# Moving one store, one mask load and eight key multiplies and transposes in a two-layer decoder kernel

## The reference

```python
k_cmp = rms_norm(compress(kc_all, prm['cw_k'][li]), prm['kn_c'][li, 0])
s = jnp.einsum('bqhgd,bnhd->bqhgn', q_blk, k_cmp).astype(jnp.float32) * ATTN_SCALE
```

## Time and profile before

| | |
|---|---|
| median of three runs | 1782.42 us (1781.62 to 1784.81) |
| the profiled execution | 1780.31 us, span 1778.4 us |
| TensorE busy | 1699.6 us (96%) |
| VectorE busy | 1102.4 us (62%) |
| ScalarE busy | 815.6 us (46%) |
| moved by DMA | 407 MB, mean 229 GB/s |
| TensorE's longest waits in total | VectorE's weight split 17.6 us, VectorE's mask addition 11.4 us |

### The profile page before, as it was taken

How to read it: one execution, slowest core, us unless ns; L and a number is a source line. 1 busy time by engine, 2 the same in 40 slices (tenths; PEclk the granted TensorE clock), 3 DMA queues, 4 the chain that set the end, 5 groups by cost and what they waited for, 6 DMA issues and landing times.

```text
span 1778.4 us, 43576 instructions
## 1 busy us (share of the span) xinstructions
PE 1699.6 (96%) x17439; PEld 1572.0 (88%) x17439; DVE 1102.4 (62%) x1902; ACT 815.6 (46%) x1707; POOL 188.0 (11%) x360
## 2 busy tenths in 40 slices
PE   6999999988999979999998999999999999989998
PEld 5899999988888779999988988888888888889998
DVE  4478888777645664355559997744565444464554
ACT  5344444444334443354575444443445545444554
POOL 3000000000000000000000003333323343300000
PEclk9999999999999989999999999999999999999999
DMA  7888888753587768678774557887777888774564
GB/s 254 303 273 278 274 268 280 237 168 107 162 278 256 253 220 306 214 246 278 244 222 136 153 163 230 253 269 232 240 223 236 281 259 262 233 244 142 155 190 133
DMA packets 287238, 407.01 MB, mean 229 GB/s; under 512 B 18655, under 2 KB 223102, under 8 KB 286022
## 3 DMA queue, kind: packets, MB, share of 16 engines
q1 hardware_dynamic: 260338, 320.52, 56.3%
q0 software_dynamic: 26624, 83.92, 14.8%
q10 hardware_dynamic: 92, 0.02, 0.0%
HBM read 391.95 MB, written 12.45 MB: 227 GB/s over the span
## 4 chain that ended last, share of the span: by engine, by line
PE 77%; DVE 16%; ACT 2%; issue 2%; DMA 2%; SPq 0%; ACTq 0%; DVEq 0%; POOLq 0%; POOL 0%
PE PJ L1882 49%; PE XB L2285 4%; PE XB L1908 4%; DVE w_low L1157 4%; PE XB L2297 2%; PE XB L2373 2%; PE XB L2163 2%; PE XB L2354 1%; DVE scr L1176 1%; PE XB L2022 1%; PE XB L2329 1%; DVE proj L1176 1%; PE XB L1925 1%; PE XB L1982 1%; ACT w_up L683 1%
## 5 line engine op out<-in xcount | busy, mean ns | idle before, releaser
L1882 PE MATMUL PJ<-xh,w_up 128*128 128x264 f32 x3072 | 921.5, 300 | 30.0 <-DVE w_low L1157 17.6
L1882 PE MATMUL PJ<-xl,w_up 128*128 128x264 f32 x3072 | 874.7, 285 | 0.0
L1882 PE MATMUL PJ<-xh,w_low 128*128 128x264 f32 x3072 | 873.8, 284 | 0.0
L1157 DVE TENSOR_TENSOR w_low<-wring,w_up 128x512 fp32r<-128x512 f32 x768 | 524.7, 690 | 407.8 <-ACT w_up L683 383.8
L683 ACT CAST w_up<-wring 128x512 fp32r<-128x512 f32 x768 | 473.6, 618 | 411.4 <-PE PJ L1882 394.3
L1882 PEld LDWEIGHTS PJ<-xh,w_up 128*128 128x128 f32 x3072 | 581.5, 189 | 52.6 <-issue 20.2
L1882 PEld LDWEIGHTS PJ<-xl,w_up 128*128 128x128 f32 x3072 | 581.0, 189 | 3.1
L1882 PEld LDWEIGHTS PJ<-xh,w_low 128*128 128x128 f32 x3072 | 578.8, 188 | 0.0
L651 POOL DMA_DIRECT2D cring<-in_cache_c_sel_kv_dram x256 | 137.3, 536 | 1314.1 <-issue 1020.2
L974 ACT COPY kcmp<-XB 128x512 f32<-128x512 f32 x80 | 46.8, 585 | 149.9 <-PE XB L2285 149.8
L1551 DVE COPY kcmp<-XB 128x512 f32<-128x512 f32 x80 | 55.3, 691 | 74.3 <-PE XB L2285 73.1
(11 more groups left out here) (328 smaller groups left out, 1501.3 us busy)
## 6 DMA issues: line engine op xcount, KB each, us to landing
wring<-in_w_in_ab_dram SPq DMA_DIRECT2D x144, 512.0 KB, 4.7
cring<-in_cache_c_cmp_kv_dram SPq DMA_DIRECT2D x128, 512.0 KB, 5.4
cring<-in_cache_c_sel_kv_dram POOLq DMA_DIRECT2D x256, 256.0 KB, 3.9
wring<-in_w_in_c_dram SPq DMA_DIRECT2D x112, 512.0 KB, 4.4
wring<-in_w_ple_gate_dram SPq DMA_DIRECT2D x64, 512.0 KB, 4.5
cring<-in_cache_a_kv_dram SPq DMA_DIRECT2D x48, 512.0 KB, 5.0
wring<-in_w_out_ab_dram SPq DMA_DIRECT2D x32, 512.0 KB, 3.8
cring<-in_cache_c_win_kv_dram POOLq DMA_DIRECT2D x64, 256.0 KB, 4.4
```

The lines of the kernel that those rows point to most:

```text
L1157: nc.vector.tensor_tensor(w_low[:, e % NE], raw(e), w_up[:, e % NE].bitcast(F32), ALU.subtract).then_inc(sem("w_lo"), 1)
L1882: ins = nc.tensor.matmul(PJ[(2 * bl + c) % 4][:, 0:T], w[:, e % NE, k, tileT(c)], x[:, kx, :], start=(kx == 0 and w is w_up and x is xh), ...
```

## The change

The store of `hs` moves from block 1's load turn to behind the loads that SP issues in block 5's turn; for that, the first of the loop's four rounds is written out on SP. The load of `mask_a` moves behind that loop. ScalarE's wait for the store goes. The key multiply of sequence b moves to slot 17 + 2b counted from m = 0 (m = 2, slots 1, 3, 5, 7; m = 3, slots 1, 3, 5, 7), its transposes to the slot after it (m = 2 slot 2 up to m = 4 slot 0), and each multiply has a mark of its own, raised by the instruction itself.

```diff
--- before.py
+++ after.py
@@ -135,7 +135,7 @@
 
 
         PE_STEPS = ("vn_made",)
-        DVE_STEPS = ("gate_scaled", "kc_ready", "qzu_set", "qzr_set", "scmp_p", "pexp_ready", "diag_set", "kcp_ready", "pc_centred", "pc_p",
+        DVE_STEPS = ("gate_scaled", "kc_ready0", "kc_ready1", "kc_ready2", "kc_ready3", "kc_ready4", "kc_ready5", "kc_ready6", "kc_ready7", "qzu_set", "qzr_set", "scmp_p", "pexp_ready", "diag_set", "kcp_ready", "pc_centred", "pc_p",
                      "sel_p", "win_p", "vnew_set")
 
         def step(name):
@@ -268,7 +268,8 @@
 
         MISC = {(0, 7): ("gate", 0), (1, 1): ("gate_T", 0), (9, 7): ("scmp", 0), (10, 3): ("psum", 0), (10, 4): ("imp", 0),
                 (11, 6): ("ptexp", 0), (14, 6): ("s_new", 0), (15, 0): ("kcp", 0), (15, 4): ("kcp_T", 0), (16, 3): ("vcp", 0)}
-        MISC.update({(3, b): ("kc_T", b) for b in range(B)})
+        KC_NORM = {divmod(17 + 2 * b, SLOTS): b for b in range(B)}
+        MISC.update({divmod(18 + 2 * b, SLOTS): ("kc_T", b) for b in range(B)})
         MISC.update({(10 + n // 2, 5 + 2 * (n % 2)): ("sum", 18 + n) for n in range(6)})
         MISC.update({at: ("nat", 4 * OUT_PAIR[n // 2][0] + 2 * OUT_PAIR[n // 2][1] + n % 2) for n, at in enumerate(
             [(12, 0), (12, 1), (12, 2), (12, 3), (13, 0), (13, 1), (13, 2), (13, 3), (14, 0), (14, 1), (14, 2), (14, 3),
@@ -461,19 +462,25 @@
                         for t in range(2):
                             sp.dma_start(p_nat[:, t, :], A["p_prompt"][0, 0, tileT(t), :]).then_inc(sem("p_in"), 16)
                         sp.dma_start(p_nat[0:B, 2, :], A["p_sample"][0].rearrange("b s d -> b (s d)")).then_inc(sem("p_in"), 16)
-                        sp.wait_ge(sem("xT_even"), KC // 2)
-                        sp.wait_ge(sem("xT_odd"), KC // 2)
-                        sp.dma_start(resid, hs).then_inc(sem("spilled"), 16)
-                    elif (bl, q) == (3, 0):
-                        sp.dma_start(mask[:, 0:M_A], A["mask_a"]).then_inc(sem("mask_a_in"), 16)
+            def block_loads(i, bl):
+
+                for q in range(1, 4):
+                    quarter(i * 4 + (4 + bl), w_ab, i + 1, bl, q)
+                quarter(i * 4 + (5 + bl), w_ab, i + 1, bl + 1, 0)
+                for n in range(NP):
+                    page(i + 1, 0, bl, n)
+
             quarter(4, w_ab, 1, 0, 0)
-            with sp.Fori(0, 4) as i:
+            for bl in range(4):
+                block_loads(0, bl)
+                if bl == 1:
+                    sp.wait_ge(sem("xT_even"), KC // 2)
+                    sp.wait_ge(sem("xT_odd"), KC // 2)
+                    sp.dma_start(resid, hs).then_inc(sem("spilled"), 16)
+            with sp.Fori(0, 3) as i:
                 for bl in range(4):
-                    for q in range(1, 4):
-                        quarter(i * 4 + (4 + bl), w_ab, i + 1, bl, q)
-                    quarter(i * 4 + (5 + bl), w_ab, i + 1, bl + 1, 0)
-                    for n in range(NP):
-                        page(i + 1, 0, bl, n)
+                    block_loads(i + 1, bl)
+            sp.dma_start(mask[:, 0:M_A], A["mask_a"]).then_inc(sem("mask_a_in"), 16)
 
             def cache_a(n):
 
@@ -770,7 +777,6 @@
                             for k in range(2):
                                 act.wait_ge(sem("pT_made"), k + 1)
                                 nc.scalar.copy(pT[:, k, :], XB[2 + k][:, 0:T]).then_inc(sem("pT_taken"), 1)
-                act.wait_ge(sem("spilled"), 16)
 
             def ab1_round(r, norm):
 
@@ -1526,11 +1532,8 @@
                 if s == 0:
                     dve.wait_ge(sem("ks_root"), 1)
                     link(nc.vector.reciprocal(krt, krt))
-                ins = nc.vector.tensor_tensor(kcmp[:, s], kcmp[:, s], krt[:, 4 * s:4 * s + 4].rearrange("p (n o) -> p n o", o=1)
-                                              .broadcast_to([P, 4, P]), ALU.mult)
-                if s == B - 1:
-                    link(ins)
-                    dve.sem_inc(step("kc_ready"), 1)
+                nc.vector.tensor_tensor(kcmp[:, s], kcmp[:, s], krt[:, 4 * s:4 * s + 4].rearrange("p (n o) -> p n o", o=1)
+                                        .broadcast_to([P, 4, P]), ALU.mult).then_inc(step(f"kc_ready{s}"), 1)
 
 
 
@@ -1707,8 +1710,8 @@
                         link(nc.vector.reciprocal(rrow[:, :], rrow[:, :]))
                     if s < 5 and 2 <= m <= 13:
                         c_norm(m - 2, s)
-                    if m == 2:
-                        kc_norm(s)
+                    if (m, s) in KC_NORM:
+                        kc_norm(KC_NORM[m, s])
                     special(m, s)
                     if taken is not None:
                         chunk_max(taken)
@@ -2202,7 +2205,7 @@
                         rows = P if c < 2 else B
                         ins = nc.tensor.transpose(XB[3][0:rows, 64 * c:64 * c + 48], gT[:, c * P:c * P + rows], ident[0:48, 0:48])
                 elif kind == "kc_T":
-                    pe.wait_ge(*done("kc_ready"))
+                    pe.wait_ge(*done(f"kc_ready{n}"))
                     for a in range(4):
                         ins = nc.tensor.transpose(XB[3][:, tileT(a)], kcmp[:, n, a, :], ident)
                 elif kind == "scmp":
```

## The result

The changed kernel took 1786.78 us (median of 19 runs, 1784.91 to 1790.09) against 1782.84 for the kernel before in the same series (19 runs): a ratio of 1.0026, 95% interval 1.0020 to 1.0032. So it became slower by some 3.6 to 5.7 us (the two medians lie 3.9 apart); forecast were +0.8, and no change within 0.2% as the likeliest. The two profiled executions are 1784.91 (span 1783.0) and 1780.31 us, 4.6 apart.

What follows compares the result with a forecast made beforehand. TensorE, busy 96% of the span, bounds the kernel, VectorE for some 80 us from 969.65; pages -1.77, copy +1.0 and keys +1.6 sum to +0.8 us, giving 1783.2 on the median, range 1779.0 to 1787.0.

Steps and rivals of the forecast that it cites:

- Where the loss shows: Second layer's blocks m = 2 and 3: VectorE idle about 1.5 us before the splits of slot 7 would show it.
- the 1.74 of before: VectorE's old idle in m = 2, 0.32 + 1.42 us, which the forecast said goes with the spread keys.
- VectorE idles 1.46 twice and 0.19 twice: Blocks m = 2 and 3: new idle 3.30 us behind multiplies 2, 6 and 0, 4; less 1.74, taken as +1.6.
- no idle: Behind multiplies 3 and 7, whose next slots belong to the next block, VectorE was to have no idle.
- the way to TensorE 0.06: First link after the 0.69 us multiply in the 2.67 us key chain: VectorE's result lets TensorE go 0.06 us later.
- Pages -1.77: 50 to 63 us: TensorE's waits of 0.78 and 0.99 us for two cache pages go when the copy leaves.
- landings come in the order of issue, the copy holds the transfers behind it: Early DMA loads: the copy of hs holds the transfers behind it for 5.7 us.
- the pages stay late: Rival, chance 0.20: VectorE's additions and SP's issue order set the two pages, gain 0; sum +2.6, 1785.0 us.
- Copy +1.0: Block 5 to 6: first weight quarter behind the copy lands at 121.5 to 122.5, ScalarE's cast late, +1.0 us.
- the copy starves block 6: Rival, chance 0.12: quarter behind the copy lands at 126.8, TensorE's block 6 waits; copy +5.9, sum +5.7, 1788.1 us.
- Mask, waits, unrolled loop: 0: Later mask load hidden (at worst +1.5), dropped wait for the copy and SP's unrolled first round: 0 us.

Runs made afterwards that it cites:

- run 3: Kernel before with the key multiplies spread as in the change, but each pair's transposes three slots behind its multiply: 1781.41 against 1782.77 us, ratio 0.9993.
- run 5: Kernel before with the key edits alone, ScalarE's copy of transposed keys behind the slot's weight cast instead of ahead: 1785.60 against 1783.76 us, ratio 1.0011.
- run 9: Kernel before with the key edits alone, TensorE transposing the identity ahead of its waits for pairs 0 and 4: 1786.39 against 1782.40 us, ratio 1.0024.
- run 10: Kernel before with the key edits alone, transposes of pairs 0 and 4 one slot later than in the change: 1786.97 against 1782.40 us, ratio 1.0030.
- run 12: Kernel before with the key edits alone, ScalarE's copy behind the cast and TensorE's waits for pairs 0 and 4 filled: 1784.81 against 1783.26 us, ratio 1.0009.
- run 13: Kernel before with the key edits alone, but each pair's transposes two slots behind its multiply: 1782.28 against 1783.26 us, ratio 0.9996.
- run 1: Kernel before with the change's key edits alone, transposes one slot behind the multiply, copy and mask unmoved: 1785.32 against 1782.77 us, ratio 1.0015.
- run 2: Kernel before with the copy and the mask load moved as in the change, keys unmoved: 1783.11 against 1782.77 us, ratio 1.0005.
- run 11: Kernel before with keys spread, transposes three slots behind, pages one quarter earlier, key multiplies on ScalarE: 1778.68 against 1782.40 us, ratio 0.9975.

## Why the prediction was wrong

**Where the loss shows: right.** It shows as idle time of VectorE. From 940 to 984 us, less the 1.74 of before, beside the measured step: changed kernel 4.27 - 1.74 = 2.53 (2.72), run 3 0 - 1.74 (-1.79), run 5 3.78 - 1.74 = 2.04 (2.31), run 9 3.82 - 1.74 = 2.08 (2.31), run 10 6.21 - 1.74 = 4.47 (4.87), run 12 3.23 - 1.74 = 1.49 (1.78), run 13 0.86 - 1.74 = -0.88 (-0.77). The row of 0.50 at the end, which run 3 shows and each of the others has, is left out. VectorE's work is the same in all of these, so its step must be, within 0.4, its idle time; that says where the loss shows, not what makes it.

**"VectorE idles 1.46 twice and 0.19 twice": the sizes in part, the mechanism half.** The price was +1.6 and the measured one +2.6 to +2.7: new idle 4.27 instead of 3.30, 0.65 more behind the multiplies 0 and 4, 0.36 behind 3 and 7, where "no idle" stood. The way over ScalarE's copy exists: run 5, which cuts it, takes 0.36 and 0.67 away. But run 5 still loses 2.31, so it is only one of two ways back to VectorE; the other runs over TensorE itself. The step that failed is "the way to TensorE 0.06": it let TensorE go on as soon as a multiply was done and never asked what TensorE did until then. VectorE's loop slot s does the split for slot s + 3, so TensorE has up to three slots of split weights in stock. A transpose one slot behind a multiply makes TensorE wait for VectorE's present place, with the stock unused: 3.38 and 1.96 us at the first pair of each block. From there on TensorE is late (in the changed kernel it works without a gap up to the next wait), ScalarE's casts and roots wait for it, and VectorE's splits for the casts. From multiply 0 to multiply 4 VectorE takes 18.06 us in the changed kernel and 15.96 in run 3, where it doesn't stand idle. By the same rows the agreement of 1.44 with 1.46 is in part luck: the transposes before it waited for TensorE, not for the multiply. Runs 1, 13 and 3 show the cost by distance; with three slots, the length of the stock, VectorE doesn't idle from 940 to 982 us. That TensorE's lateness is the link is read from the profile (in run 5 the casts and roots wait for it) and was not tried by itself.

**"Pages -1.77": wrong, -0.3 on the profiled pair and nothing in the mean of the profiles.** The failed step is "landings come in the order of issue, the copy holds the transfers behind it", applied to pages that were issued 13.5 and 16.7 us after the copy and so 3.5 and 6.7 us after it had landed. The rival "the pages stay late" was the true one: with the copy moved the waits are as long as without (0.88 and 0.88 us in the mean), and SP issues the pages late; with an earlier issue all three profiles show no wait. The size was wrong as well: 1.77 is the highest of nine profiles with the copy in its old place.

**"Copy +1.0": right, +0.90 and +0.87.** The quarter landed at 121.7, as forecast, and was waited for 6.0 us. The Trainium skill (DMA: Bandwidth & Descriptors, "Two DMAs through the same engine are not ordered") would have allowed it to land ahead of the copy; here it landed 1.5 us behind. The rival "the copy starves block 6" did not come.

**Mask, waits, unrolled loop: 0, right.** From 200 to 590 us the changed kernel's step is +0.02.

**The sum.** On the profiled pair: forecast -1.77 + 1.0 + 1.6 = +0.8; measured -0.3 + 0.9 + 2.7 = +3.3, and +1.3 from places that the change doesn't touch (597, 665, 1540 to 1600 and the start). The medians of runs 1 and 2, 2.55 + 0.34 = 2.9, lie 1.0 below the changed kernel's 3.9, which their intervals allow. The two terms that failed, pages and keys, make 1.5 and 1.1 of the difference on the pair.

## What to carry to other kernels

A slot in the written order is not a moment: where a producer's queue runs some slots ahead, a consumer placed fewer slots behind than that lead can have to stand still with its stock unused. Here one slot cost 2.59 us, two gained 0.77 and three, the lead, gained 1.79. Look at the lead before choosing the distance, and look first whether the queue that you relieve has anything waiting in it. Where a waiting engine's clock falls, fill the wait before blaming the clock: here that gave back 0.28 of 2.59.

## What was not expected of the hardware

The granted clock near 597 us: TensorE waits 2.22 or 2.23 us there in each of the fifteen profiles, and behind that wait the clock fell to 0.50 in twelve of them and not in three (the kernel before twice, and run 10). The fall is a step of 1.5 us, and of 2.9 in run 13, where the clock stood at 0.50 from 598 to 604 us. In the same way the first 30 us differ by up to 4 us between profiles. The length of a wait alone doesn't decide it in these traces: in run 11 the clock fell behind waits of 1.07 and 0.51 us (mean 0.72 from 946 to 952), and in run 13 it stayed at 1.00 there behind one of 1.93. What decides either stays open. Both mean that a loss or a wait read off one profile has to be seen in a second.
